# Narrow products of a two-block transformer kernel: the narrow weights made stationary, 256 tokens moving, the result turned by two transposes

## The reference, cut to what matters

```python
h = rmsnorm(x, norm_mix_w[l])
proj = h @ w_in[l]
q, k, v, z, xbc, dt_raw, gates = jnp.split(proj, split_at, axis=-1)   # dt_raw: 16 columns
...
dt = jax.nn.softplus(dt_raw.reshape(b, s, 2, SSD_HEADS).astype(f32) + dt_bias.astype(f32))
...
h2 = rmsnorm(x, norm_ffn_w[l])
# in hierarchical_moe, t = h2 as 256 tokens:
p_group = jax.nn.softmax((t @ w_rg + b_rg).astype(jnp.float32), axis=-1)   # 4 columns
fine = (t @ w_re + b_re).astype(jnp.float32).reshape(-1, N_EXPERT_GROUPS, EXPERTS_PER_GROUP)  # 16 columns
```

## Time and profile before

| | us |
|---|---|
| median of 3 runs | 1723.48 |
| the runs | 1721.24, 1723.48, 1724.27 |
| span of the profiled execution | 1719.7 |
| PE busy | 1580.2 (92%) |
| DVE busy | 1107.8 (64%) |
| ACT busy | 859.1 (50%) |
| mean granted TensorE clock | 0.958 |

### The profile page before, as it was taken

The page is one execution under the profiler, slowest core; times in us unless marked ns, Lnnn a source line. Parts: engine busy times, 40 slices in busy tenths (PEclk is TensorE's granted clock), DMA queues, the critical chain, the costliest instruction groups (busy, mean ns, idle before and its releaser), DMA issues.

```text
span 1719.7 us, 24221 instructions
## 1 busy us (share of the span) xinstructions
PE 1580.2 (92%) x8754; PEld 1299.4 (76%) x8754; DVE 1107.8 (64%) x1811; ACT 859.1 (50%) x1397; POOL 13.2 (1%) x36
## 2 busy tenths in 40 slices
PE   5989989899999999899669999797888799999999
PEld 3855557888888888777559999685666788889788
DVE  3546654654444456679977676686565769687795
ACT  4335554622222227588865554634342558556572
POOL 2000000000000000000000000000000000000000
PEclk9999999899999999999879999899899799999999
DMA  9388731423333322332326666442220479788792
GB/s 337 102 333 311 278 121 51 147 74 97 94 93 96 96 88 72 99 90 82 122 75 196 185 182 194 123 135 86 74 74 25 158 280 332 273 288 317 261 362 104
DMA packets 195802, 279.71 MB, mean 163 GB/s; under 512 B 12435, under 2 KB 111221, under 8 KB 190589
## 3 DMA queue, kind: packets, MB, share of 16 engines
q1 hardware_dynamic: 194308, 274.21, 47.8%
q0 software_dynamic: 1152, 4.19, 0.6%
q10 hardware_dynamic: 248, 0.09, 0.0%
HBM read 277.40 MB, written 1.05 MB: 162 GB/s over the span
## 4 chain that ended last, share of the span: by engine, by line
PE 70%; DVE 15%; ACT 8%; issue 3%; DMA 2%; SPq 0%; POOL 0%; DVEq 0%; ACTq 0%; POOLq 0%
PE bank L433 61%; DVE weights_lo L406 3%; ACT weights_hi L394 2%; DMA ada_rows_in<-in_ada_w_dram 1%; PE bank L707 1%; PE bank L1314 1%; DVE work L2643 1%; ACT act_hi L501 1%; PE bank L1298 1%; PE bank L1282 1%; ACT turn L505 1%; DVE work L2680 1%; DVE work L2690 1%; ACT work L2014 1%; DVE x_and_ctx L2643 1%
## 5 line engine op out<-in xcount | busy, mean ns | idle before, releaser
L406 DVE TENSOR_TENSOR weights_lo<-stage,weights_hi 128x1024 fp32r<-128x1024 f32 x332 | 394.5, 1221 | 78.3 <-ACT weights_hi L394 74.2
L394 ACT ACTIVATE weights_hi<-stage 128x1024 fp32r<-128x1024 f32 x332 | 337.6, 1056 | 149.6 <-PE bank L433 99.1
L433 PE MATMUL bank<-act_hi,weights_hi 128*128 128x256 f32 (+1 forms) x1040 | 330.2, 318 | 17.9 <-DVE weights_lo L406 9.6
L433 PE MATMUL bank<-act_lo,weights_hi 128*128 128x256 f32 (+1 forms) x1040 | 328.1, 316 | 0.0
L433 PE MATMUL bank<-act_hi,weights_lo 128*128 128x256 f32 (+1 forms) x1040 | 328.0, 315 | 0.0
L433 PEld LDWEIGHTS bank<-act_hi,weights_hi 128*128 128x128 f32 x1040 | 203.2, 195 | 32.8 <-DVE weights_lo L406 11.3
L433 PE MATMUL bank<-weights_hi,ff_hi 128*128 128x512 f32 x560 | 219.4, 392 | 1.9 <-DVE ff_lo L2852 1.9
L433 PE MATMUL bank<-weights_hi,act_hi 128*128 128x512 f32 (+1 forms) x488 | 196.9, 403 | 24.6 <-DVE act_lo L2704 16.0
L433 PE MATMUL bank<-weights_hi,ff_lo 128*128 128x512 f32 x560 | 219.0, 391 | 0.0
L433 PE MATMUL bank<-weights_lo,ff_hi 128*128 128x512 f32 x560 | 218.5, 390 | 0.0
L433 PEld LDWEIGHTS bank<-act_lo,weights_hi 128*128 128x128 f32 x1040 | 203.2, 195 | 11.5
(11 more groups left out here) (395 smaller groups left out, 2051.2 us busy)
## 6 DMA issues: line engine op xcount, KB each, us to landing
stage<-in_mlp_w_dram SPq DMA_DIRECT2D x128, 512.0 KB, 4.0
stage<-in_w_dram SPq DMA_DIRECT2D x96, 512.0 KB, 5.8
ada_rows_in<-in_ada_w_dram SPq DMA_DIRECT2D x40, 1024.0 KB, 5.8
x_and_ctx<-in_w_dram SPq DMA_DIRECT2D x48, 512.0 KB, 5.7
work<-in_w_dram SPq DMA_DIRECT2D x48, 512.0 KB, 6.0
stage<-in_w_in_dram SPq DMA_DIRECT2D x32, 512.0 KB, 4.3
stage<-in_lru_w_in_dram SPq DMA_DIRECT2D x20, 512.0 KB, 4.4
stage<-in_attn_w_qkv_dram SPq DMA_DIRECT2D x12, 512.0 KB, 8.1
```

The lines of the kernel that those rows point to most:

```text
L394: act.eng.activation(whi[u % NRING][:], landing(act, u)[:], ACT.Copy).then_inc(sem("hi_ready"), 1)
L406: dve.eng.tensor_tensor(wlo[u % NRING][:], landing(dve, u)[:], whi[u % NRING][:].bitcast(F32), ALU.subtract).then_inc(sem("lo_ready"), 1)
L433: m = pe.eng.matmul(ps, l, r, start=start and j == 0, stop=stop and j == 2, skip_group_check=True)
```

## The change

Both products are turned round. The narrow weights are now stationary and all 256 tokens move, so each product is 24 matmuls in place of 48, and its result stands with the 16 or 20 columns on partitions. ACT copies these rows to SBUF (`dt_rows`, `router_rows`, in the tile named `turn`), and two transposes on PE turn them back to tokens on partitions, in the form in which DVE read them before. Each stationary block is 80 columns wide (`NARROW`): a block begins at its own 16 or 20 columns and runs on into the neighbour's, and the extra rows of the result are not read. Both weights lie in one tile `w_small` with 60 zeroed columns behind, and are split by two DVE instructions instead of four.

Four orders change with it. The router's matmuls wait, tile k by tile k, for the low part of the second 128 tokens. The transposes of `dt` stand on PE behind those of the keys and ahead of `xbc(4)`, and wait for ACT's copy. ACT's copy for the router stands between its two `xn_hi`. DVE's second `xn_lo` moves from ahead of the bias to behind the first part of the router's arithmetic. The rest of the diff:

```diff
+        NARROW = 80
+        WSMALL = KT * 36 + NARROW - 20
+        wsm = sb("w_small", [P, WSMALL])
+        wsm_hi = sb("w_small_hi", [P, WSMALL], F32R)
+        wsm_lo = nc.alloc_sbuf_tensor_at("w_small_lo", [P, WSMALL], F32R, offset=slab["w_small"])
...
+        dt_rows, router_rows = tbuf[0:16, 1, 0:TX], tbuf[0:20, 0, 0:TX]
...
-            def small_product(key, bank, pitch, cols, wh, wl, ready=None):
+            def small_product(key, bank, n, first, ready=None):
+                if plan.uses[bank]:
+                    t.wait_ge(*pe.bank_free(bank))
+                ps = pe.take((key, "wide"), bank)
+                for k in range(KT):
+                    if ready:
+                        t.wait_ge(*ready(k))
+                    at = slice(first + n * k, first + n * k + NARROW)
+                    mm = three(pe, ps[0:NARROW, 0:TX], wsm_hi[:, at], wsm_lo[:, at], hh_(k), hl_(k), k == 0,
+                               k == KT - 1, True)
+                mm.then_inc(*pe.fill((key, "wide")))
+
+            def small_turn(key, bank, n, rows, pitch):
+                t.wait_ge(*pe.freed((key, "wide")))
                 if plan.uses[bank]:
                     t.wait_ge(*pe.bank_free(bank))
                 ps = pe.take(key, bank)
                 for tt in TWO:
-                    if ready:
-                        t.wait_ge(*ready(tt))
-                    tok = slice(tt * P, (tt + 1) * P)
-                    for k in range(KT):
-                        mm = three(pe, ps[:, tt * pitch:tt * pitch + cols], wh[:, k, :], wl[:, k, :],
-                                   hhi[:, k, tok], hlo[:, k, tok], k == 0, k == KT - 1, False)
+                    mm = t.transpose(ps[:, tt * pitch:tt * pitch + n], rows[:, tt * P:(tt + 1) * P], ident[0:n, 0:n])
                 mm.then_inc(*pe.fill(key))
...
-            small_product("dt", 2, 16, 16, wdt_hi, wdt_lo)
+            small_product("dt", 2, 16, 0)
...
             mm.then_inc(*pe.fill("turnk"))
+            small_turn("dt", 2, 16, dt_rows, 16)
             xbc(4)
...
-            small_product("router", 0, 32, 20, wrt_hi, wrt_lo, lambda tt: turned_at("n3", "lo", tt, KT - 1))
+            small_product("router", 0, 20, KT * 16, lambda k: turned_at("n3", "lo", 1, k))
+            small_turn("router", 1, 20, router_rows, 32)
...
             xbc_tap(3)
+            s.wait_ge(*act.filled(("dt", "wide")))
+            s.activation(dt_rows, plan.bank(("dt", "wide"))[0:16, 0:TX], ACT.Copy).then_inc(*act.free(("dt", "wide")))
...
-            for tt in TWO:
-                s.activation(XNH[:, tt, :], xn0[:, tt, :], ACT.Copy).then_inc(*act.mark("xn_hi"))
+            s.activation(XNH[:, 0, :], xn0[:, 0, :], ACT.Copy).then_inc(*act.mark("xn_hi"))
+            s.wait_ge(*act.filled(("router", "wide")))
+            s.activation(router_rows, plan.bank(("router", "wide"))[0:20, 0:TX],
+                         ACT.Copy).then_inc(*act.free(("router", "wide")))
+            s.activation(XNH[:, 1, :], xn0[:, 1, :], ACT.Copy).then_inc(*act.mark("xn_hi"))
...
+            v.memset(wsm[:, KT * 36:WSMALL], 0.0).then_inc(*dve.mark())
...
-            for hi, w, lo in ((wdt_hi, wdt, wdt_lo), (wrt_hi, wrt, wrt_lo)):
-                v.tensor_copy(hi[:], w[:]).then_inc(*dve.mark())
-                v.wait_ge(*dve.own())
-                v.tensor_tensor(lo[:], w[:], hi[:].bitcast(F32), ALU.subtract).then_inc(*dve.mark())
+            v.tensor_copy(wsm_hi[:], wsm[:]).then_inc(*dve.mark())
+            v.wait_ge(*dve.own())
+            v.tensor_tensor(wsm_lo[:], wsm[:], wsm_hi[:].bitcast(F32), ALU.subtract).then_inc(*dve.mark())
```

More of the change, by code:

```diff
@@ L240, in build @@
         dts = sb("dt_cols", [P, 3, 2, 16])
[L241 to L245, removed]
+        NARROW = 80
[3 more added lines that the diff above has]
+        wsm_lo = nc.alloc_sbuf_tensor_at("w_small_lo", [P, WSMALL], F32R, offset=slab["w_small"])
+        wdt = wsm[:, 0:KT * 16].rearrange("p (k n) -> p k n", k=KT)
+        wrt = wsm[:, KT * 16:KT * 36].rearrange("p (k n) -> p k n", k=KT)
         dta_hi, dta_lo = sb("dta_hi", [P, 2, 16], F32R), sb("dta_lo", [P, 2, 16], F32R)
@@ L1062, in small_loads @@
                 e.dma_start(small[:, a:a + n], src.to_broadcast([P, n])).then_inc(sem("smalls"), 16)
-            e.dma_start(wdt[:], w_in_2[0].rearrange("(k p) n -> p k n", p=P)[:, :, 2048:2064]).then_inc(
+            e.dma_start(wdt, w_in_2[0].rearrange("(k p) n -> p k n", p=P)[:, :, 2048:2064]).then_inc(
                 sem("w_small"), 16)
@@ L2998, in first_max, with xn_low @@
                 v.wait_ge(*dve.own())
-            for tt in TWO:
+            def xn_low(tt):
                 v.wait_ge(sem("xn_hi"), tt + 1)
@@ L3003, in _ @@
                                 ALU.subtract).then_inc(*dve.mark("xn_lo"))
+            xn_low(0)
             L, group, o1, weight = rt(0, 2, 20), rt(2, 2, 4), rt(3, 2, 4), rt(4, 2, 4)
@@ L3022, in _ @@
             v.wait_ge(*dve.own())
+            xn_low(1)
             v.wait_ge(*dve.filled("count"))
```

## The result

The changed kernel takes 1715.86 us (median of five runs, 1714.74 to 1717.58), the kernel before in the same comparison 1723.48 (five runs, 1721.24 to 1725.81). The medians are 7.6 us apart. The ratio is 0.995, 95% interval 0.9936 to 0.9964, that is 8.6 us less, with 6.2 and 11.0 as ends. The forecast was 4.9 us less: the direction was right, the size too small.

The account below looks back on a forecast made before the run. PE was taken as the bound, busy 92% of the span with 70% of the last-ended chain. Router 3.7 plus attention 1.2 made 4.9 us off 1719.7, so 1714.8, plus 3.8 gave 1718.6 us, range 1715.7 to 1722.3.

Parts of the forecast that it names:

- The router's steps: At the router: 24 matmuls replace 48, plus ACT's copy and two transposes; product's end 1344.1 against 1347.82, gain 3.7 us.
- the forecast's 5 and 45: Router product in the kernel before: five matmuls start at clock 1.00, the other 45 run at 0.50 in 9.14 us.
- The time-step steps: At `dt`: product gains nothing itself; `xbc(4)` starts two us later, at 1145.9, and the delay fills PE's idleness before 1163.05.
- the term: Attention: with PE's idleness nearly gone, the clock may not fall at 1164.4; 1.2 us gained, bounds nothing and 1.7.
- all that is saved here should pass on to the end: Behind the router, logits, counts, expert order and first expert's DMA wait in turn, so its 3.7 us should reach the end.
- I take nothing: Counts behind the router: at full clock their 2.31 us shrink, but only 0.7 could come out; counted as nothing.
- Rival 1: Larger gain: full clock for most of the router product (5.4), counts 0.7, attention 1.7; 7.8 us, 1715.7; chance 0.12.
- Rival 2: Small gain: router product cold throughout (2.8), attention's clock falls or `xbc(4)` costs DVE tenths; 2.5 us, 1721.0; chance 0.25.
- Rival 3: Slower: 80-column stationary blocks load slowly, router 4.6 us slower, 1728; chance 0.05 together with slower through `dt`'s transposes.
- Rival 4: Slower: `dt`'s transposes hold up PE, delaying `xbc(4)` and gates, 1725; chance 0.05 together with slower through narrow block loads.

Follow-up runs that it names:

- e4: Kernel before with 18 unused matmuls on PE behind the gate units of the first attention block: 1723.8 us, ratio 0.9989.
- e3: Changed kernel with the two transposes of `dt` behind `xbc(5)`, so PE doesn't wait for ACT's copy: 1719.93 us, ratio 0.997.
- e5: Kernel before with nine small DVE operations, a delay of 1.8 us, between the counts and the order of the experts: 1724.42 us, ratio 1.0001.
- e6: Changed kernel with nine small DVE operations, a delay of 1.8 us, between the counts and the order of the experts: 1720.08 us, ratio 0.9972.
- e9: Changed kernel with 29 unused matmuls around the router's, to have its clock at 1.00: 1716.25 us, ratio 0.9951.
- e12: Kernel before with seven unused matmuls in each of PE's two pauses in the expert stage: 1722.14 us, ratio 0.9992.
- e13: Changed kernel with unused matmuls around the router's and seven in each of the expert stage's two pauses: 1712.81 us, ratio 0.9935.
- e1: Kernel before with the router's part of the change alone, `dt` keeping its old product on the packed weights: 1718.11 us, ratio 0.9956.
- e7: Changed kernel with stationary blocks of 128 columns in place of 80: 1714.16 us, one execution.
- e8: Changed kernel with stationary blocks of 64 columns in place of 80: 1719.61 us, one execution.

## Why the forecast fell short

**Step by step.** The router's steps held. In times of the kernel before (0.63 added) the product started at 1338.63 (forecast 1338.5) and ended at 1343.5 (1343.1): 20 matmuls started at half clock in place of 16. That this came so close was in part luck. The forecast let the clock fall as the product began and stay at half for 3.4 us; it fell 2.7 us earlier and stayed for 6.8. ACT's copy took 0.38 (0.42), the two transposes 0.31 (0.5), and the logits came at 1344.4 (1344.1). So 3.55 us where 3.7 was forecast. In all five other profiles with the old product that stretch took 15.89 and not 15.38 us, and the gain is 4.05: there all 48 matmuls start at half clock, while in the first profile of before the clock fell only after six of them, and 42 started at half (the forecast's 5 and 45 add up to 50, since a window also counts what still runs at its edge). The second `xn_lo` ended at 1346.94 in the time of the changed kernel, 0.28 ahead of the read of the counts: no cost.

The time-step steps held as well, in the changed kernel's own time: copy at 1144.85 (1144.95), `xbc(4)` at 1145.64 (1145.9), no wait of DVE, and the pause of 3.15 us shrunk to 0.48. The clock does not fall at 1164 in any of the eight profiles with the new `dt` in its place, nor in e4; it does in all five with the old one and no fillers there, and in e3. But the term was counted to 1.2 us as if nothing followed. In five of those eight a stretch of 6.8 us at half clock comes at 1187 to 1190 in its place, and on the average attention takes 60.50 us against 61.26 with the old `dt`: 0.8 us. The three without it had the shortest pause ahead of the second block's scores, 0.48 to 0.58 us, the five with it 0.78 to 0.96. Nor was the 1.7 us for the clock's fall at 1164 the usual price: it stands for 3.4 us at half clock, which only the first profile of before had.

**The step that failed** is the end of the reading of the router, "all that is saved here should pass on to the end", with the sum closed at the logits. It passed on with more. First, "I take nothing" for the counts: from the logits to the order it is 5.08 us on the average of six profiles against 5.39, 0.3 us. Second and mostly, the expert stage. Without a delay or fillers of its own it took 351.10, 351.17, 352.72 and 352.73 us with the old router, mean 351.9, and 349.55 to 349.60 in all six with the new one: 2.4 us, and 1.5 in the pair of first profiles. e5, e6 and e9 move the stage by 2 us and switch the stretch off or on; e12 and e13 fill the pauses and it is gone. Summed on the averages: 4.05 + 0.3 + 0.8 + 2.4 = 7.5 us, beside 7.6 between the medians and 8.6 by the ratio, whose interval (6.2 to 11.0) holds both. The same terms without attention, 6.7 us, meet e1 (6.6 between the medians, 7.6 by the ratio).

The trace had half of this within the forecast's reach. The reasoning that was used at 1164, a pause of PE and then 3.4 us at half clock, would have found the same at 1505, and with it 1.5 us that could be won; only the two places of the change were read. That the change would win them could not be read from one profile.

**The rivals.** Rival 1 had the size (7.8 us) by other means: the clock was not full in the product (20 matmuls start at 0.50), the counts gave 0.3, not 0.7, and attention 0.8, not 1.7. Rival 2 fell: the product wasn't at half clock throughout, and `xbc(4)` cost DVE nothing. Rival 3 fell by e7 and e8: the step is 0.21 us at half clock and 0.12 at full for 64, 80 and 128 columns. The rule of the Trainium skill, "TensorE: Matmul & The Clock Gate", section "Weight-path perf modes", that fast loading wants 128 columns has nothing to act on here: the 128-column load took 330 ns at half clock, as many ns for each further column as the narrower ones. The same section's sentence that fp32 gains nothing by it is the one that agrees. Rival 4 fell: `dt`'s transposes made PE wait 1.2 us and started `xbc(4)` 1.8 us later, inside its cover, and in e3, without that wait, the kernel was slower by 3 us, as far as two intervals that just overlap can say.

**What stays open.** Why a pause of 1.8 us is followed by half clock in one kernel and not in another is only shown as a matter of when it comes. That the new router's timing avoids it in six profiles of six, the old one's in none of four, is shown; a kernel with other work ahead of the stage may have it the other way. What the traces add is that the timing repeats: in the six, the logits come 8.4 to 8.6 us after the clock's fall at the router, and with the old product 12.5 to 12.7 us in five profiles and 9.4 in the first profile of before. This fits the equal results, but no run tests it. The 0.5 us of the gather differ from profile to profile (14.78 to 15.26) and aren't the change's.

## What to carry to other kernels

A narrow product whose few columns move is paid by the matmul: with the weights stationary and the tokens moving, half the matmuls did the same work at nearly the same step (0.21 us at half clock in both forms, 0.12 against 0.11 at full), and two small transposes and a copy cost 0.7 us. A forecast of a shift must be carried through the stages behind it: list PE's pauses there that stand next to a stretch of half clock, since a saving of 2 to 4 us can win or lose 1.5 us at each. Where such pauses remain, fill them before judging small edits, or a good edit can show no gain (e9).

## What the runs showed of the hardware

- A pause of PE of 1.8 us between stretches of full load was followed by 3.4 us at half clock or by none, with identical work around it: in 6 of the 13 profiles without fillers there at one or both of two places. Each such stretch cost 1.5 to 1.6 us (349.6, 351.1, 352.7). With seven unused matmuls in the pause it was gone in both kernels tried.
- A wait can pay: with PE held up by 1.2 us behind `dt` the clock stayed at 1.00 at 1164, nineteen microseconds later, and taking that wait away (e3) cost some 3 us by the ratios and 3.3 in attention.
- 24 matmuls with 64, 80 or 128 stationary columns under 256 moving ones took 4.82, 4.89 and 4.85 us, while a load took 223, 250 and 330 ns at half clock.
- In the first profiles the new router product reached 2.4 GHz after 20 of its 24 matmuls; the old one started its last 42 of 48 at 0.50 and never came back to 2.4 GHz.
